# Eight low-part subtractions of the input projection go from VectorE to GpSimd, and one small subtraction is made later

## The reference, cut to what matters

```python
h_l = rmsnorm(x_l, norm_g[l]) * (1.0 + sc) + sh
u_l = h_l @ w_in[l]
...
h = jnp.sin(freq * (feats @ w1 + b1))
h = jnp.sin(freq * (h @ w2 + b2))        # filter hidden layer
h = (h @ w3).astype(f32).reshape(L, 2, 2, HY_W)   # taps, times a decay
k = k * lax.rsqrt(jnp.sum(k * k, axis=0, keepdims=True) + EPS)
return jnp.fft.rfft(k, axis=0)
```

## Time and profile before

| | |
|---|---|
| three runs | 907.92, 909.27, 909.46 us; median 909.27 |
| profiled execution | 909.16 us, of it 907.4 us span |
| busy | PE 889.1 us, DVE 695.2, ACT 427.4, POOL 199.1 |
| `w_lo`, L1590 | 68 instructions, 91.2 us, mean 1341 ns |
| chain that ended last | PE 85%, DVE 6%, DMA 4%, ACT 3% |

### The profile page before, as it was taken

One profiled execution on the slowest core, in us unless ns is written; L12 is line 12 of the kernel. 1 busy time (PEld: TensorE's weight loads), 2 busy tenths in 40 slices (PEclk: granted clock), 3 DMA queues, 4 the chain that ended last, 5 costly groups with the idle time before them and its releaser, 6 DMA issues.

```text
span 907.4 us, 12258 instructions
## 1 busy us (share of the span) xinstructions
PE 889.1 (98%) x4750; PEld 739.3 (81%) x4750; DVE 695.2 (77%) x860; ACT 427.4 (47%) x635; POOL 199.1 (22%) x167
## 2 busy tenths in 40 slices
PE   9999999999999999999999999999999999999996
PEld 6777777678888888888888888989898988888885
DVE  5555896789997789967786585678686787869796
ACT  4655565534434544333324342555464456635464
POOL 1222300310002200001001773100100201495651
PEclk9999999999999999999999999999999999999999
DMA  9999942335473354478776242775667534875854
GB/s 358 418 416 421 397 178 70 105 100 191 140 186 99 99 149 170 170 216 329 286 287 216 75 149 95 170 233 150 124 182 196 100 142 187 306 240 187 232 185 186
DMA packets 37173, 184.67 MB, mean 204 GB/s; under 512 B 4443, under 2 KB 5851, under 8 KB 27004
## 3 DMA queue, kind: packets, MB, share of 16 engines
q1 hardware_dynamic: 32816, 147.84, 44.1%
q0 software_dynamic: 3968, 35.65, 16.0%
q10 hardware_dynamic: 332, 0.40, 0.1%
HBM read 177.98 MB, written 37.75 MB: 238 GB/s over the span
## 4 chain that ended last, share of the span: by engine, by line
PE 85%; DVE 6%; DMA 4%; ACT 3%; issue 2%; SPq 0%; POOL 0%; DVEq 0%; ACTq 0%
PE pp L2367 38%; PE pp L2683 17%; PE pp L2397 17%; PE pp L2284 3%; DMA ada_raw<-in_w_ada_dram 3%; PE pp L2260 3%; PE pp L2649 2%; PE pp L2640 1%; PE pp L2641 1%; PE pp L2290 1%; DVE softmax_stats L1875 1%; DMA ada_raw<-in_w_scale_dram 0%; DVE pt_lo L1890 0%; ACT U L1162 0%; PE pp L2466 0%
## 5 line engine op out<-in xcount | busy, mean ns | idle before, releaser
L2367 PE MATMUL pp<-h_hi,w_hi 128*128 128x512 f32 x544 | 214.0, 393 | 2.4 <-ACT UG L1242 1.4
L2367 PE MATMUL pp<-h_hi,w_lo 128*128 128x512 f32 x544 | 212.5, 391 | 0.0
L2367 PE MATMUL pp<-h_lo,w_hi 128*128 128x512 f32 x544 | 212.3, 390 | 0.0
L1590 DVE TENSOR_TENSOR w_lo<-w_raw,w_hi 128x1024 fp32r<-128x1024 f32 x68 | 91.2, 1341 | 71.0 <-ACT w_hi L939 70.3
L939 ACT ACTIVATE w_hi<-w_raw 128x1024 fp32r<-128x1024 f32 x68 | 71.8, 1056 | 132.0 <-PE pp L2367 131.9
L2367 PEld LDWEIGHTS pp<-h_hi,w_hi 128*128 128x128 f32 x544 | 102.6, 189 | 24.3 <-issue 2.9
L2367 PEld LDWEIGHTS pp<-h_hi,w_lo 128*128 128x128 f32 x544 | 102.5, 188 | 21.7
L2367 PEld LDWEIGHTS pp<-h_lo,w_hi 128*128 128x128 f32 x544 | 102.6, 189 | 20.6
L2683 PE MATMUL pp<-wo_hi,side_hi 128*128 128x512 f32 x224 | 87.3, 390 | 0.1
L2683 PE MATMUL pp<-wo_hi,side_lo 128*128 128x512 f32 x224 | 87.2, 389 | 0.0
L2683 PE MATMUL pp<-wo_lo,side_hi 128*128 128x512 f32 x224 | 87.1, 389 | 0.0
(11 more groups left out here) (364 smaller groups left out, 1945.2 us busy)
## 6 DMA issues: line engine op xcount, KB each, us to landing
w_raw<-in_wb_dram SPq DMA_DIRECT2D x68, 512.0 KB, 3.8
ada_raw<-in_w_ada_dram SPq DMA_DIRECT2D x15, 2048.0 KB, 12.7
w_out_sums<-in_w_out_dram POOLq DMA_DIRECT2D x16, 1024.0 KB, 9.7
w_gate_raw<-in_w_gate_dram SPq DMA_DIRECT2D x16, 1024.0 KB, 7.2
wo_raw<-w_out_sums SPq DMA_DIRECT2D x16, 1024.0 KB, 4.9
wo_raw<-in_w_out_dram SPq DMA_DIRECT2D x12, 1024.0 KB, 4.9
wa_raw<-in_wa_dram SPq DMA_DIRECT2D x18, 288.0 KB, 7.7
UG<-in_xT_dram SPq DMA_DIRECT2D x7, 512.0 KB, 8.7
```

The source lines that it names most:

```text
L1590: eng.tensor_tensor(lane(wb_lo, n % KW), lane(wb_raw, n % KW), lane(wb_hi, n % 2), ALU.subtract).then_inc(wb_lo_done, 1)
L2367: mm = eng.matmul(ps[i][:], w, x, start=(kk == 0 and m == 0), stop=(kk == KT - 1 and m == 2))
```

## The change

`POOL_LOWS` lists the chunks whose low part POOL makes: 1 to 5 ahead of the first sum of squares, 6, 7 and 8 ahead of the second, third and fourth. DVE makes the low parts of chunk 0 and of 9 to 67. Both waits now hold `wb_lo_done >= n`, which keeps the counter in order across the two engines. The low part of `h2` moves on DVE from step 0 to step 2 of the loop, behind the last `h_lo` and `shifted`, and SP's load of `last_raw`, which waits for it, moves behind the load of chunk 4.

```diff
+POOL_LOWS = ((1, 2, 3, 4, 5), (6,), (7,), (8,))
@@ sync
                 slot = n - 2
-                if slot == 1:
+                if slot == 2:
                     eng.wait_ge(mlp_sin, 4)
                     eng.dma_start(last_raw[:], t["tables"][:, 2048:2304]).then_inc(tab_in, 16)
@@ gpsimd
+            def chunk_low(n):
+                eng.wait_ge(wb_hi_done, n + 1)
+                eng.wait_ge(wb_lo_done, n)
+                eng.tensor_tensor(lane(wb_lo, n % KW), lane(wb_raw, n % KW), lane(wb_hi, n % 2), ALU.subtract).then_inc(wb_lo_done, 1)
+
             for o in range(2):
                 for l in range(4):
+                    if o == 0:
+                        for n in POOL_LOWS[l]:
+                            chunk_low(n)
                     eng.wait_ge(taps_sq, 4 * o + l + 1)
@@ vector
             def chunk_low(n):
                 eng.wait_ge(wb_hi_done, n + 1)
+                eng.wait_ge(wb_lo_done, n)
@@
-                if n + 1 < 4 * B_GROUPS:
+                if POOL_LOWS[-1][-1] < n + 1 < 4 * B_GROUPS:
                     chunk_low(n + 1)
@@
-                if n == 0:
+                if n == 2:
                     eng.wait_ge(mlp_sin, 3)
                     eng.tensor_tensor(h2[64:128, :], sines[1], h2[0:64, :], ALU.subtract).then_inc(mlp_sin, 1)
```

## The result

| | before | after |
|---|---|---|
| runs | 7, median 908.83 us (907.92 to 909.46) | 7, median 911.67 us (910.51 to 912.50) |
| profiled execution | 909.16 us, span 907.4 | 911.87 us, span 910.1 |
| POOL busy | 199.1 us | 222.5 us |

The ratio after/before is 1.0031, 95% interval 1.0019 to 1.0042: 2.8 us slower, where 0.5 was forecast. The time, 911.67 us, lies inside the stated range (906.8 to 912.4 us) and above the forecast's own, narrower one (908.6 to 911.0 us).

What follows compares the result with a forecast made beforehand. PE, busy 98% of the span, was taken as the bound. Tokens 0.1, `filter_hidden` 0.1 and taps 0.25, rounded up to +0.5 us on 909.16, gave 909.7, as median 909.8 us; own range 908.6 to 911.0, stated range 906.8 to 912.4.

Steps and rivals of the forecast that it cites:

- POOL's price: A low-part subtraction on POOL was taken to last 2.40 us, against 1.14 us taken off DVE's list.
- DVE's standstill: DVE instructions with two SBUF inputs stand still while POOL works, ending their own length less 0.2 us after POOL.
- the new waits: New PE waits for `w_lo` were foretold ahead of chunks 6 and 7, in the taps stage.
- the second rival: POOL's subtraction takes longer, delaying L(2), L(3) and the chain L(6) to L(8): 912.2 us at 2.75 us each; chance 0.16.
- The first rival: The shared port does not hold DVE up, so the taps stage gains 3.5 us: 905.8 us; chance 0.15.
- L(1) and L(4): Low parts of chunks 1 and 4, on POOL; L(4) was foretold done near 148.2 us, wanted at 149.9.
- Tokens: Ahead of chunk 3, the last `h_lo` ends at 141.6 to 141.8 us, wanted at 141.7: loss 0 to 0.4, taken 0.1.
- `filter_hidden`, SP and ACT: Ahead of chunk 4, the later `last_raw` lets ACT finish at 149.2 us against 149.07: loss 0 to 1.1, taken 0.1.
- L(6), L(7), L(8): Low parts of chunks 6 to 8 on POOL, taps stage: balances 0, -0.5 and finally +0.25 us at spectrum 3.
- PE's clock: The profiled execution's stretch at 1.2 GHz after the column sums cost 1.6 us; the sum added no term for it.
- The third rival: Waits at chunks 7 and 8 bring a second slow-clock stretch, or ACT's later copy a longer one: 911.5 us; chance 0.06.

Runs made afterwards that it cites:

- the run with the fills: Changed kernel with each of POOL's eight subtractions replaced by three zero fills of the same buffer, low parts of chunks 1 to 8 left out of the result; 905.88 us.
- chunks 6 to 8 alone: Changed kernel with POOL making only the low parts of chunks 6 to 8 and `filter_hidden` in its old place; median 909.59 us, ratio 1.0008.
- the clock kept: Changed kernel with seven unused matmuls on PE behind the column sums, ahead of chunk 4; median 909.69 us, ratio 1.0014.
- the earlier copy: Changed kernel with ACT copying PE's bank before making `last_hi` and `fwd_hi`; median 910.22 us, ratio 1.0014.
- the kernel with the low parts in the gap: Kernel before with DVE making low parts of chunks 6 to 8 between L1646 and L1649, where it waited for ACT; medians 906.08 and, on another chip, 905.43 us.

## Why the prediction was nearly right, and what it missed

The mechanism held: POOL's price, DVE's standstill, and the places of the new waits. The size did not: +2.8 us where +0.5 was forecast. That the time is inside the stated range is in part luck. The range reached to 912.4 us to cover the second rival, longer subtractions that delay the chain through chunks 6 to 8, and that rival is not what made the kernel slow. (Its own figure is off too: a price of 2.3 us on the median of before, 909.27, gives 911.6 and not 912.2 us.) Two of the marks that the prediction set were missed: the first product of slice 3 starts at 186.98 and spectrum 3 at 192.05, foretold for 184.5 and 189.5 to 190. Of the lateness 2.2 us had come about before the taps stage: with the tokens, at chunk 4 and through the clock.

- *POOL's price and DVE's standstill:* right. 2.36 to 2.42 us at the least; `h_tmp`, L1656 and L1629 stretched as foretold, and the run with the fills shows the cause. The first rival, that the port does not hold DVE, gave 905.8 us from an execution with the slow stretch; the run with the fills comes near to that case and took 905.88, its stretch at 1.2 GHz 3.4 us long, as in the kernel before. The second rival's longer subtraction came in part: six of eight took 2.75 us or less, L(1) and L(4) 3.23 and 3.42, and PE waited for neither.
- *Tokens, 0.1 us:* the last `h_lo` was foretold for 141.6 to 141.8 and ended at 141.90; PE lost 0.36 us. Within the bounds of 0 to 0.4, but at the end that was not chosen.
- *`filter_hidden`, SP and ACT, 0.1 us:* **the step that failed.** `filter_hidden` ended at 145.24 as foretold (145.0), but `last_raw` then took 3.3 us instead of 2.4 and ACT's chain ran to 150.3 instead of 149.2. A slack of 4.31 us was spent down to nothing, and PE waited 0.73 us more. The sum counted to 149.2 against 149.07, which left no margin for a load that landed 0.9 us later, and it took the near end of 0 to 1.1 us.
- *L(6), L(7), L(8), +0.25 us:* right in mechanism. The new waits stand at chunk 6 (0.35 after, 0.58 with chunks 6 to 8 alone; foretold 0.6) and chunk 7 (1.20; foretold about 1.0), L1629 is held and slice 3 starts late. The wait for spectrum 3 is 1.39 us (foretold 1.5). The size is 0.4 to 0.6 us by the traces, and 0.1 to 0.6 by the levels of the run with them alone.
- *PE's clock:* the sum put it at nothing, and it is the second term that failed. The third rival named "ACT's later copy" as a cause of a longer stretch and gave it 0.06. It came, 3.4 us longer, by clock and time in three of seven executions. What no step had was that the stretch of before was itself a matter of chance, there in 38 of 72 executions. The changed kernel had it in all seven.
- *The sum:* waits of 1.65 us by the levels (910.95 against 909.3) and 1.8 with the clock kept; by the rows of the traces 1.55, of it 0.36 tokens, 0.73 ACT, 0.46 taps. To that the clock adds 0.47 x 1.35 = 0.6 us for the free executions that are gone and 3/7 x 1.2 = 0.5 for the long ones: together 2.65 to 2.9, measured 2.8. The part of the clock is made from the levels of the same runs, so this says how the loss divides and is no second proof of its size. That the long stretch hangs on PE's longer wait follows from two edits that each took it away, the earlier copy and the matmuls (in none of 20 executions, against three of seven); what exactly the clock reacts to stays open.

The longer landing of `last_raw` is not explained. It was 2.0 us in the kernel before with the late `filter_hidden`, and 3.0 to 3.3 in three kernels, all with the late `filter_hidden` and POOL's subtractions, where SP issues its second load of a chunk 2.5 us behind it. That second load is hardly the cause: it starts at 147.8, when a landing in 2.4 us would have been over (147.7). None of this was tried.

## What to carry to other kernels

A subtraction moved from VectorE to GpSimd is not free for VectorE: count on its instructions with two inputs in SBUF to stand still for GpSimd's whole 2.4 us, twice VectorE's own 1.2, and look first for an idle gap on VectorE itself, here the 1.2 us in which it waited for ScalarE. When an instruction is moved later, follow it through the DMA to the engine in whose list its consumer stands, and book a slack used up to the last tenth as a loss. Where an engine's clock can fall, one profiled execution is one draw: time the kernel before often enough to see whether its times have two groups before pricing a change of 0.1%.

## What the hardware showed that was not expected

- TensorE's clock behind sixteen one-column matmuls and 0.85 us of idling fell to 1.2 GHz for 3.4 us in one profiled execution of the kernel with the low parts in the gap, and stayed at 2.4 GHz in the other; by the run times of the kernel before it falls in about half. Four to seven 128-column matmuls in the idle time kept it up in the profiles of both kernels, and by the times in all 21 executions. With 1.58 us of idling it was low for 6.8 us in the profiled execution.
- A zero fill of 128x1024 on GpSimd takes 0.95 us and leaves VectorE alone; a subtraction of that size takes 2.4 and holds it.
- Where both engines have SBUF work in a row they hold each other up: `h_lo` x2 took 3.25 us and the GpSimd subtraction beside it 3.23, against 1.4 and 2.4 alone.
